# Two sets of 256 tokens for the last MLP tile and the norm between two blocks, with half of the value rows ahead of the forget gates

## The reference

```python
y_x = _sq_relu_mlp(_modulate(x, g_pre_mlp[l], sh2, sc2), w_mlp_in[l], w_mlp_out[l])
x = x + gt2 * _rmsnorm(y_x, g_post_mlp[l])      # end of the first block
...
h = rmsnorm(x, norm_mix[l])                     # start of the second
proj = h @ w_in[l]
c_q, c_kv, k_rope, hq, hf, hi, hg, mq = [proj[..., offsets[j]:offsets[j + 1]] for j in range(len(IN_SIZES))]
...
f = lbf + (1.0 - lbf) * jax.nn.sigmoid(f_raw.astype(f32))   # f_raw is hf
k = 1.0 - f
logf = jnp.log(f)
v = i_raw.astype(f32)                                       # i_raw is hi
```

## Time and profile before

| | |
|---|---|
| median of 3 runs | 1413.1 us (1411.2 to 1416.69) |
| profiled execution | 1411.99 us, span 1410.7 us |
| PE, PEld busy | 1354.0 us (96%), 1077.4 us (76%) |
| DVE, ACT, POOL busy | 596.9, 547.7, 660.5 us |
| mean granted TensorE clock | 0.991 |

### The profile page before, as it was taken

The page is one execution under the profiler, slowest core; times in us unless marked ns, Lnnn a source line. Parts: engine busy times, 40 slices in busy tenths (PEclk is TensorE's granted clock), DMA queues, the critical chain, the costliest instruction groups (busy, mean ns, idle before and its releaser), DMA issues.

```text
span 1410.7 us, 16178 instructions
## 1 busy us (share of the span) xinstructions
PE 1354.0 (96%) x6476; PEld 1077.4 (76%) x6476; DVE 596.9 (42%) x864; ACT 547.7 (39%) x870; POOL 660.5 (47%) x342
## 2 busy tenths in 40 slices
PE   7999999899999999997999999999999999999999
PEld 4687667778888888885778787666677888888887
DVE  4797786653200142005648565845442221022210
ACT  4522675355332343223444536634363322132321
POOL 3544326754444444554478672633244444444442
PEclk9999999999999999998999999999999999999999
DMA  9575234343233333332221111121032323333331
GB/s 381 199 281 191 76 139 179 105 120 103 91 92 102 98 101 94 103 94 77 85 75 61 45 61 60 46 60 35 26 105 79 101 90 105 99 95 90 105 95 70
DMA packets 40651, 148.59 MB, mean 105 GB/s; under 512 B 4224, under 2 KB 4480, under 8 KB 39808
## 3 DMA queue, kind: packets, MB, share of 16 engines
q1 hardware_dynamic: 39696, 144.26, 31.5%
q0 software_dynamic: 448, 2.62, 0.5%
q10 hardware_dynamic: 432, 0.67, 0.1%
HBM read 144.65 MB, written 2.10 MB: 104 GB/s over the span
## 4 chain that ended last, share of the span: by engine, by line
PE 77%; DVE 11%; POOL 5%; ACT 4%; issue 3%; DMA 0%; DVEq 0%; POOLq 0%; ACTq 0%
PE bank L550 22%; PE bank L552 21%; PE bank L551 21%; POOL wL L2440 2%; PE bank L602 2%; POOL EE L2590 2%; DVE macc L1811 1%; PE bank L618 1%; PE bank L590 1%; PE bank L592 1%; PE bank L591 1%; DVE acc L2139 1%; DVE small L1961 1%; PE bank L925 1%; PE bank L633 1%
## 5 line engine op out<-in xcount | busy, mean ns | idle before, releaser
L2440 POOL TENSOR_TENSOR wL<-raw,wH 128x1024 fp32r<-128x1024 f32 (+1 forms) x205 | 500.3, 2442 | 582.9 <-ACT wH L1198 580.8
L550 PE MATMUL bank<-hH,wH 128*128 128x512 f32 x784 | 320.1, 408 | 14.7 <-DVE hL L2133 8.4
L551 PE MATMUL bank<-hL,wH 128*128 128x512 f32 x784 | 308.6, 394 | 0.0
L552 PE MATMUL bank<-hH,wL 128*128 128x512 f32 x784 | 308.0, 393 | 0.0
L1198 ACT ACTIVATE wH<-raw 128x1024 fp32r<-128x1024 f32 (+1 forms) x205 | 215.0, 1050 | 191.3 <-PE bank L552 154.7
L550 PEld LDWEIGHTS bank<-hH,wH 128*128 128x128 f32 x784 | 149.2, 190 | 56.3 <-DVE hL L2133 11.5
L552 PEld LDWEIGHTS bank<-hH,wL 128*128 128x128 f32 x784 | 148.9, 190 | 32.4
L551 PEld LDWEIGHTS bank<-hL,wH 128*128 128x128 f32 x784 | 149.1, 190 | 28.2 <-issue 1.7
L550 PE MATMUL bank<-gH,wH 128*128 128x512 f32 x352 | 137.6, 391 | 0.0
L552 PE MATMUL bank<-gH,wL 128*128 128x512 f32 x352 | 137.0, 389 | 0.0
L551 PE MATMUL bank<-gL,wH 128*128 128x512 f32 x352 | 137.0, 389 | 0.0
(11 more groups left out here) (354 smaller groups left out, 2004.8 us busy)
## 6 DMA issues: line engine op xcount, KB each, us to landing
raw<-in_wall SPq DMA_DIRECT2D x205, 512.0 KB, 3.6
rows<-in_wall SPq DMA_DIRECT2D x24, 1024.0 KB, 10.4
bra<-in_rpbw SPq DMA_DIRECT2D x8, 360.0 KB, 4.4
xq<-in_xt SPq DMA_DIRECT2D x2, 1024.0 KB, 7.1
xT<-in_xn SPq DMA_DIRECT2D x1, 2048.0 KB, 7.9
out_x<-xT SPq DMA_DIRECT2D x8, 256.0 KB, 2.1
vE<-in_ctxt SPq DMA_DIRECT2D x1, 1024.0 KB, 19.7
icn<-in_invc POOLq DMA_DIRECT2D x1, 1024.0 KB, 8.9
```

What stands on the lines that cost most here:

```text
L550: matmul(o, a_h, b_h, start=first, stop=False)
L551: matmul(o, a_h, b_l, start=False, stop=False)
L552: return matmul(o, a_l, b_h, start=False, stop=last)
L2440: tt(wL[i % NHL][:, 0:n], raw[i % NRAW][:, 0:n], wH[i % NHL][:, 0:n].bitcast(F32), ALU.subtract).then_inc(s.w_lo, 1)
```

## The change

Four things change.

1. The last tile of `w_mlp_out` (m = 7) goes by two sets of 256 tokens, 48 matmuls of 256 columns each, into two banks. The squares of tile 7 are no longer added by POOL: PE sums `acc` and the square of tile 7 (`half_statistic`), once for each set. The root of the first set is made while PE is still in the second set. The second norm then goes over eight feature blocks for the first set and again for the second. DVE makes the scaling and the sum in PSUM banks 0 and 5; ACT writes the high part and copies the sum to `xT`; POOL takes no part. The squares for the next norm go to `y`, and PE adds them (`four_sums`, eight matmuls of 32 rows in all) inside the group of gates, where the statistic `h3` now is too.
2. The value rows of the first two sets of 128 tokens stand ahead of the gates, the other two where they were. The four chunks of these weights are therefore loaded and split twice (209 chunks in all). The act-table load and one of the copies that stood behind the values are moved: one ahead of the last splits, one gone to the first pass.
3. The eight `late_column(5, k)` move from tile 7 of `w_out` to tile 4 of `w_mlp_in`, and DVE reads them there.
4. The calls `ahead("w_out", ...)` inside the attention loop reach the chunk of k = 4 at i = 13 (before, none past k = 2).

```diff
             tile("w_mlp_out", m, range(16 * half, 16 * half + 16))
+    wide("w_in_2", 14, range(8))
     group([("w_in_2", m) for m in (10, 11, 12, 13)], range(8))
...
-    turn(*(("w_in_2", m) for m in (10, 11, 12, 13, 6, 7, 8, 9)), *(("vt", i) for i in range(4)))
...
+    turn(("w_mlp_out", 16), ("vt", 0), ("vt", 1))
+    of.update((("w_in_2", m), b) for m, b in zip((10, 11, 12, 13, 6, 7, 8, 9), (2, 3, 4, 6, 0, 4, 1, 2)))
+    of.update({("vt", 2): 5, ("vt", 3): 6})
...
-            tile("w_out", m, range(8), [(claim(BANK["w_out", m]), MX)],
-                 beside=(lambda k: late_column(5, k)) if m == 7 else None)
+            tile("w_out", m, range(8), [(claim(BANK["w_out", m]), MX)])
...
-                tile("w_mlp_in", m, range(8), [(claim(BANK["w_mlp_in", m]), X2)])
+                tile("w_mlp_in", m, range(8), [(claim(BANK["w_mlp_in", m]), X2)],
+                     beside=(lambda k: late_column(5, k)) if m == 4 else None)
...
-            for m in range(8):
+            for m in range(8 - half):
...
-        pe.wait_ge(s.add_g, ADD_G.f + 7)
-        statistic("post_mlp", [(acc[0][:, :], 0, 128)])
+        def half_statistic(i):
+            o = claim(7)[:, 256 * i:256 * i + 256]
+            pe.wait_ge(s.add_g, ADD_G.f + 6)
+            pe.wait_ge(s.sq, SQ.f + 8 + i)
+            matmul(o, ones[:, :], acc[0][:, 256 * i:256 * i + 256], start=True, stop=False)
+            matmul(o, ones[:, :], tm[3][:, 256 * i:256 * i + 256], start=False, stop=True).then_inc(s.summed, 1)
+            freed[7] = s.root, logged(("post_a", "post_b")[i])
+
+        for i in range(2):
+            b = BANK["w_mlp_out", 15 + i]
+            o = claim(b)[:, 256 * i:256 * i + 256]
+            for k in range(16, 32):
+                w_h, w_l, raise_ = weights("w_mlp_out", k, 7)
+                x_h, x_l, sem, value = XB(k)
+                mm = products(o, w_h, w_l, x_h[:, 256 * i:256 * i + 256], x_l[:, 256 * i:256 * i + 256], k == 16, k == 31)
+                if i and raise_:
+                    mm.then_inc(s.product, 1)
+                if (i, k) == (1, 20):
+                    half_statistic(0)
+            if i == 0:
+                mm.then_inc(s.y_part, 1)
+            freed[b] = s.y_full, 8 + i
+
...
+            return hH[:, k, :], hL[:, k, :], s.lo, LO.h3 + 8 + k + 1
+
+        def other_half(k, i):
+            if (k, i) == (0, 1):
+                half_statistic(1)
+
+        rows("w_in_2_first", 14, range(8), tokens(hH, hL, X3A, 2), [claim(BANK["vt", i]) for i in range(2)], other_half)
+        for i in range(2):
+            freed[BANK["vt", i]] = s.vt_a, i + 1
...
+        def norm_statistic(k, i):
+            if (k, i) in ((3, 3), (5, 3)):
+                four_sums(1, y, SQ.h3, (k - 3) // 2)
+            if (k, i) == (6, 3):
+                pe.wait_ge(s.add_v, ADD_V.h3 + 1)
+                statistic("h3", [(tm[2][:, :], 0, 128)])
...
-        group(fs, range(8), X3)
+        group(fs, range(8), X3, norm_statistic)
+        freed[1] = s.add_v, ADD_V.h3 + 1
+        for b in (0, 5):
+            freed[b] = s.lo, LO.h3 + 16
...
-            if h == 0:
-                pe.wait_ge(s.add_v, ADD_V.h3 + 7)
-                statistic("h3", [(acc[1][:, :], 0, 128)])
-        rows("w_in_2", 14, range(8), tokens(hH, hL, X3, 4), [claim(BANK["vt", i]) for i in range(4)])
-        for i in range(4):
-            freed[BANK["vt", i]] = (s.vt_a if i % 2 else s.vt_v), i // 2 + 1
+        rows("w_in_2", 14, range(8), tokens(hH, hL, X3, 4)[2:], [claim(BANK["vt", i]) for i in (2, 3)])
+        freed[BANK["vt", 2]] = s.vt_v, 1
+        freed[BANK["vt", 3]] = s.vt_a, 3
...
             if i in (5, 9, 13):
-                ahead("w_out", (i - 5) // 4, 0, 1)
+                ahead("w_out", (i - 5) // 2, 0, 1)
...
-                for k in range(16 * half, 16 * half + 16):
+                for k in range(16 * half, 16 * half + (1 if half and m == 7 else 16)):
...
+                    elif m == 7:
+                        room(3)
+                        square(tm[3][:, 0:256], y[:, 7, 0:256], s.sq)
...
-        act.wait_ge(s.mk_n, 4)
-        root("post_mlp", 1024, rs[1])
+        root("post_a", 1024, bank[1], 256)
...
+        def second_norm(i, j):
+            t = slice(256 * i, 256 * i + 256)
+            b = bank[(0, 5)[j % 2]][:, 0:256]
+            act.wait_ge(s.add2, 8 * i + j + 1)
+            copy(hH[:, j, t], b, s.hi, vc("norm_mix_2", j))
+            copy(xT[:, j, t], b, s.x_copied)
+
+        def second_square(j):
+            act.wait_ge(s.x_copied, 8 + j + 1)
+            act.wait_ge(s.post2, 8 + j + 1)
+            square(y[:, j, :], xT[:, j, :], s.sq)
+
         for j in range(8):
-            act.wait_ge(s.add2_g if j % 2 else s.add2_v, j // 2 + 1)
-            copy(hH[:, j, :], xT[:, j, :], s.hi, vc("norm_mix_2", j))
+            second_norm(0, j)
             if j == 0:
-                act.wait_ge(s.summed, summed("mem"))
-                square(acc[1][:, :], xT[:, 0, :], s.sq)
-            else:
-                t = 2 + j % 2
-                if j == 1:
-                    act.wait_ge(s.add_g, ADD_G.f + 7)
-                room(t)
-                square(tm[t][:, :], xT[:, j, :], s.sq)
-                held[t] = s.add_v, ADD_V.h3 + j
-            if j % 2:
-                ahead("w_in_2", j - 1, 10)
+                ahead("w_in_2_first", 2, 14, 1)
+            if j == 1:
+                act.wait_ge(s.y_full, 9)
+                square(tm[3][:, 256:512], y[:, 7, 256:512], s.sq)
+                ahead("w_in_2_first", 4, 14, 1)
+            if j == 3:
+                ahead("w_in_2_first", 6, 14, 1)
+            if j == 5:
+                root("post_b", 1024, STAT[:, 256:512], 256, 256)
+            if j == 6:
+                ahead("w_in_2", 0, 10, 1)
+        for j in range(8):
+            second_norm(1, j)
+            if j == 0:
+                ahead("w_in_2", 2, 10, 1)
+                act.wait_ge(s.product, done("w_in_2_first", 7, 17))
+                for i in range(2):
+                    copy(vt[:, i, :], bank[BANK["vt", i]], s.vt_a)
+            if j == 1:
+                ahead("w_in_2", 4, 10, 1)
+            if j == 4:
+                ahead("w_in_2", 6, 10, 1)
+            second_square(j)
         ahead("w_in_2", 7, 13)
...
-                root("h3", 1024, rsx)
+                root("h3", 32 * 1024, rsx)
...
+        nc.scalar.preload_act_table_set("natural_log_exp_and_others")
...
         act.wait_ge(s.product, done("w_in_2", 7, 17))
-        for i in (1, 3):
-            copy(vt[:, i, :], bank[BANK["vt", i]], s.vt_a)
-        nc.scalar.preload_act_table_set("natural_log_exp_and_others")
+        copy(vt[:, 3, :], bank[BANK["vt", 3]], s.vt_a)
...
-        late_vector(5)
...
+                if m == 5:
+                    late_vector(5)
...
-        dve.wait_ge(s.root, rooted("post_mlp"))
+        def last_tile(i):
+            t = slice(256 * i, 256 * i + 256)
+            if i == 0:
+                dve.wait_ge(s.y_part, 1)
+                dve.wait_ge(s.y_half, 8)
+            else:
+                dve.wait_ge(s.product, done("w_mlp_out", 31, 7))
+            tt(y[:, 7, t], y[:, 7, t], bank[BANK["w_mlp_out", 15 + i]][:, t], ALU.add).then_inc(s.y_full, 1)
+
+        def second_norm(i):
+            t = slice(256 * i, 256 * i + 256)
+            root_ = STAT[:, t] if i else bank[1][:, t]
+            dve.wait_ge(s.root, rooted(("post_a", "post_b")[i]))
+            for n in range(9):
+                if n < 8:
+                    b = bank[(0, 5)[n % 2]][:, 0:256]
+                    if 8 * i + n >= 2:
+                        dve.wait_ge(s.lo, LO.h3 + 8 * i + n - 1)
+                    else:
+                        dve.wait_ge(s.y_full, 6)
+                    dve.wait_ge(s.y_full, 8 + i)
+                    stt(out=b, in0=y[:, n, t], scalar=coef[:, 4, n:n + 1], in1=root_, op0=ALU.mult,
+                        op1=ALU.mult).then_inc(s.post2, 1)
+                    dve.wait_ge(s.post2, 8 * i + n + 1)
+                    tt(b, xT[:, n, t], b, ALU.add).then_inc(s.add2, 1)
+                if n:
+                    j = n - 1
+                    dve.wait_ge(s.hi, HI.h3 + 8 * i + j + 1)
+                    dve.wait_ge(s.x_copied, 8 * i + j + 1)
+                    stt(out=hL[:, j, t], in0=bank[(0, 5)[j % 2]][:, 0:256], scalar=vc("norm_mix_2", j),
+                        in1=hH[:, j, t].bitcast(F32), op0=ALU.mult, op1=ALU.subtract).then_inc(s.lo, 1)
+                if i == 0 and n == 2:
+                    last_tile(1)
+
+        last_tile(0)
...
+        second_norm(0)
+        second_norm(1)
+        for i in range(2):
+            dve.wait_ge(row_in[i], 16 * (sum(ROW_SIGNAL[q] == i for q in ROW_PLACE) + 1))
+            nc.vector.tensor_copy(hm[:, 4 * i:4 * i + 4, :].rearrange("p l t -> p (l t)"),
+                                  tm[i][:, :]).then_inc(s.masks, 1)
+        dve.wait_ge(s.sq_sum, SQ_SUM.h3 + 2)
+        nc.vector.tensor_copy(tm[2][:, :], bank[1]).then_inc(s.add_v, 1)
...
```

(14 more changed lines are left out.)

75 lines of the change are left out of this document (31 added, 44 removed).

## The result

The changed kernel takes 1400.0 us (median, 1399.19 to 1401.78 over four runs), the kernel before, on the same chips, 1412.77 (1411.2 to 1416.69). The ratio is 0.9907 with a 95% interval of 0.9885 to 0.993, so the change brings 10 to 16 us; 1401.0 was forecast. The profiled execution has a span of 1400.5 in the place of 1410.7, and a mean granted clock of 0.995.

The account below looks back on a forecast made before the run. PE was taken as the bound, busy 1354.0 of 1410.7 us, so only its waits and slow clock could be won. Terms -4.5, -0.6 and -7.0 sum to -12.1: execution 1399.9, median 1401.0, range 1394 to 1409.

Parts of the forecast that it names:

- Part 3: Eight columns moved out of `w_out`: PE's wait for `macc` and some lower clock go, -4.5, between -4.5 and 0.
- Part 4: `w_out` chunk split in the attention loop: removes PE's 2.07 wait, adds 1.5 in the loop; -0.6, between -2.1 and +1.4.
- the loop's loss: Attention loop: one more split on ACT and POOL makes PE wait longer for `P`, +1.5, bounds 0 and 3.5.
- The transition: Last MLP tile to first product on `EE`: work 74.1 plus waits 7.4 against 88.6; -7.0, bounds -14.5 and 0.
- the last tile's +0.6: Last tile of `w_mlp_out`: 96 matmuls of 256 columns take 11.5 in place of 10.9.
- The first pass: Norm of the first 256 tokens: ACT slowest by a little, 1.43 per block; PE waits 1.9 in the value rows.
- the gates' start: Second norm pass, beside the gates: no wait of PE but 0.9 at the start of the gates.
- the second value rows: Value rows behind the queries: PE waits about 2.9 and 1.0 for POOL's second and third weight chunks.
- The first product on `EE`: Start of the recurrence: POOL reaches `EE` at 725.4, before 732.44; PE has it at 727.7, before 734.75.
- The rival of POOL slowing DVE: First pass: POOL's four splits slow DVE's operations, 8.8 in all; gain only 3.3, 1410; chance 0.08.
- The slow first pass: First pass: blocks take DVE and ACT 1.9, not 1.43; PE waits 4 more; gain 8.1, 1405; chance 0.15.
- The clock as a rival: First-pass value rows and gates: short waits put PE on its lower clock, +15.4 to +33, 1416 to 1433; chance 0.02.

Follow-up runs that it names:

- e1: Kernel before with only the eight `late_column(5, k)` moved from tile 7 of `w_out` to tile 4 of `w_mlp_in`; ratio to the kernel before 0.9958.
- e10: Kernel before with both the eight columns moved and the `w_out` chunk of k = 4 split in the attention loop; ratio to the kernel before 0.9953.
- e2: Kernel before with only the `w_out` chunk of k = 4 split inside the attention loop; ratio to the kernel before 0.9986.
- e3: Changed kernel with the column move and the extra `w_out` split taken back; last tile, norm and values stay changed; ratio to the kernel before 0.9942.
- e4: Changed kernel with ACT's splits of the second and third value chunks moved forward among the `Silu` of the queries; ratio to the kernel before 0.9882.
- e7: e4 with the third chunk's split ahead of the third `Silu` and the fourth's ahead of the last; ratio to the kernel before 0.9875.
- e6: Changed kernel, passes of 256 tokens kept, but all four sets of value rows behind the queries; ratio to the kernel before 0.9956.
- e5: Changed kernel with DVE's two results of each norm step in `y` and `xT` instead of the banks; ratio to the kernel before 0.996.
- e8: Changed kernel with one more ACT copy of 256 columns for each block of the first pass; ratio to the kernel before 0.9917.
- e9: e7 with the `w_out` chunk's splits on ACT and POOL later in the attention loop; median 1392.17 us, ratio to the kernel before 0.9855.

## Why the prediction was right

**Part 3.** Forecast -4.5, measured -4.70 at the last tile (e1). The wait was as read in the list, the columns cost the same in both places, and DVE's sums have some 50 us of cover at the new one.

**Part 4.** Forecast -0.6, from -2.07 and +1.5. Measured -1.1 behind part 3 (e10 against e1, drift taken off) and -0.2 alone (e2). The size of the loop's loss was near the estimate, 1.27, but its mechanism was not the one given: not ACT's split ahead of the exponentials, but POOL's split beside DVE's scaling of `P`, 1.96 for 0.49. The prediction weighed POOL slowing DVE for the passes alone; it happened here. The gain in `w_out` was 0.3 larger than the wait, and not by a low clock: there was none there. That the columns would take most of the gain, were they left where they are, was not in the working; it did no harm, because part 3 took them away.

**The transition.** Forecast -7.0, measured -6.9 (e3: -6.4 alone). By steps: the last tile's +0.6 and the half statistics hold (12.4 for 12.2). The first pass was given 1.9 of wait and had 0.5 ahead of the statistic and little else on the list; the gates' start, 0.9, has 0.3 there. With what a restart costs beside the wait, the stretch from the first value row to the gates took 13.1, and 13.6 was forecast. The `four_sums` and the statistic inside the gates were right, and no wait for `hL` stands in the gates. In the second value rows 2.9 + 1.0 for two chunks was forecast, and there are 0.79, 1.98 and 0.54 for three. By the prediction's own times its two chunks are the third and the fourth, which it calls second and third. The sum, 3.3, is near, and the cause, ACT's order, is what e4 and e7 removed. The first product on `EE` came with its chain: POOL begins it at 720.24. Of the 6.9, 1.7 lies behind the value rows: from their end to the first product pass 6.5 before and 4.8 now. PE's wait of 1.47 for `vt` is gone there, with a table load and a copy of ACT moved out of the way. No run takes these moves back by themselves; e6, which has the table load moved and the copies as before, needs 5.4.

**The rival of POOL slowing DVE** was kept out for the reason given: a bank operand. e5 is the counter-proof, 8.3 for a price of 8.8. The slow first pass did not occur, but e8 shows it 0.7 us of ACT's time away. The clock as a rival: it did not fall at the value rows (1.00 in the gates). It fell elsewhere, in the recurrence, and took 2.8 from the profiled execution, 1.3 of it by way of DVE beside POOL. The last tile's weight loads are 0.19 long at a pitch of 0.12, and the tile took what its pitch says. The sentence of the Trainium skill that a load overlaps with matmuls in flight only when the row group differs ("TensorE: Matmul & The Clock Gate", The mechanism) is contradicted once more; the same section also lets a load into the background weight buffer go ahead, and no run shows whether these are such loads.

Forecast in all -12.1, measured -12.8 between the medians (10 to 16). The parts in the traces, without drift, are 4.7, 1.1 and 6.9, in all 12.7; that the sum agrees so closely is in part luck, since part 4 is off by 0.5 and the low clock in the recurrence, worth up to 2.9, was in no term.

## What to carry to other kernels

A norm between two products costs PE its whole latency unless PE has work that needs only a part of the tokens. Splitting the norm in two gives nothing by itself; it is the work on the first part that hides the second, and DVE's results must lie where POOL's splits don't stop DVE. The same holds for where a split is placed: look at what DVE does beside it before blaming the engine whose queue it stands in. A wait that is removed ahead of another wait may bring little: follow what starts the engine that ends the second one, and what the clock does behind it, and remove the last one first. When a weight chunk serves for half the time, look at where its split stands in the in-order queue of the engine that makes it: moving three of ACT's splits brought the first product on `EE` 4.4 us forward here.

## What was not expected of the hardware

One same wait of PE, 2.04 for a root in the recurrence, stands in the profiled executions of all twelve kernels. In five (before, e2, e3, e4, e9) the granted clock behind it is 1.00 over four us and nothing is lost. In the other seven it fell: in e1, e6 and e7 1.0 is lost up to the next waits for `EE`, and in the changed kernel, e5, e8 and e10 2.9, with a DVE addition on `PX` beside POOL's split taking 2.3 in the place of 1.1. So one profiled execution can misstate a change by 2.9 us, more than part 4 is worth, and places in the trace ahead of such a fall compare better than spans do. What decides whether it falls these runs don't tell. The Trainium skill ("TensorE: Matmul & The Clock Gate", Part 1: The HAM clock gate) says of the start of a kernel that the number of slow matmuls differs from run to run; here that shows in the middle of one, behind a short wait.

A column of one element, beside matmuls of 512, costs 0.23 us of PE (a pitch of 0.91 for three matmuls and a column, three matmuls being 0.68), as much as one of those matmuls.

One operand in SBUF and none in a bank is not enough to keep DVE clear of POOL: the scaling of `P`, with a single SBUF tensor as its input, took 1.96 beside a split and 0.49 without.
